# SwiGLU activations of an FFN turned in 32x32 blocks by VectorE and placed through DRAM, instead of by TensorE

## The reference, cut to what matters

```python
mix = jnp.concatenate([ret, moba], axis=-1) @ w_out[layer]
x = x + rmsnorm(mix, post_mix_norm[layer])
h = rmsnorm(x, pre_ffn_norm[layer])
f = (jax.nn.silu(h @ w_gate[layer]) * (h @ w_up[layer])) @ w_down[layer]
x = x + rmsnorm(f, post_ffn_norm[layer])
```

## Time and profile before

| | |
|---|---|
| median of 3 runs | 305.52 us (305.44 to 305.65) |
| profiled execution | 305.34 us, of it a span of 303.5 us |
| mean granted TensorE clock | 0.997 |
| TensorE busy | 98% of the span |
| VectorE, ScalarE busy | 61%, 51% |
| DMA | 58.35 MB, mean 192 GB/s |

### The profile page before, as it was taken

How to read it: one execution, slowest core, us unless ns; L and a number is a source line. 1 busy time by engine, 2 the same in 40 slices (tenths; PEclk the granted TensorE clock), 3 DMA queues, 4 the chain that set the end, 5 groups by cost and what they waited for, 6 DMA issues and landing times.

```text
span 303.5 us, 4145 instructions
## 1 busy us (share of the span) xinstructions
PE 296.3 (98%) x1440; PEld 240.2 (79%) x1440; DVE 183.9 (61%) x273; ACT 155.5 (51%) x255; POOL 12.0 (4%) x20
## 2 busy tenths in 40 slices
PE   8999999999999999999999999999999999999992
PEld 3788877787888888887888888888888888888881
DVE  2867466796877879797456464546355464551146
ACT  4989476736482747495253353544352443630331
POOL 0030000000020013200000000000000000000001
PEclk9999999999999999999999999999999999999998
DMA  6999986218627441669846454654746454600003
GB/s 189 404 408 381 409 353 203 74 31 302 199 94 265 122 168 59 219 204 384 304 148 211 159 197 143 209 190 160 253 139 243 155 219 132 212 6 0 0 2 138
DMA packets 17545, 58.35 MB, mean 192 GB/s; under 512 B 2003, under 2 KB 2556, under 8 KB 17532
## 3 DMA queue, kind: packets, MB, share of 16 engines
q1 hardware_dynamic: 17136, 57.06, 53.4%
q0 software_dynamic: 304, 1.06, 1.0%
q10 hardware_dynamic: 92, 0.05, 0.1%
HBM read 57.10 MB, written 1.06 MB: 192 GB/s over the span
## 4 chain that ended last, share of the span: by engine, by line
PE 87%; DVE 7%; DMA 2%; ACT 1%; issue 1%; SPq 0%; DVEq 0%; POOL 0%; ACTq 0%
PE bank L978 26%; PE bank L980 26%; PE bank L979 26%; PE bank L988 3%; DVE w_lo L887 3%; DMA xT<-in_xt 2%; PE bank L1018 1%; PE bank L1022 1%; PE bank L1026 1%; PE bank L1087 1%; PE bank L1132 1%; DVE d_lo L894 1%; PE bank L997 1%; DVE res L969 1%; DVE res L963 1%
## 5 line engine op out<-in xcount | busy, mean ns | idle before, releaser
L978 PE MATMUL bank<-w_hi,a_hi 128*128 128x512 f32 x256 | 101.0, 395 | 0.0
L980 PE MATMUL bank<-w_hi,a_lo 128*128 128x512 f32 x256 | 99.9, 390 | 0.0
L979 PE MATMUL bank<-w_lo,a_hi 128*128 128x512 f32 x256 | 99.6, 389 | 0.0
L978 PEld LDWEIGHTS bank<-w_hi,a_hi 128*128 128x128 f32 x256 | 48.1, 188 | 10.4 <-issue 0.7
L980 PEld LDWEIGHTS bank<-w_hi,a_lo 128*128 128x128 f32 x256 | 48.0, 188 | 10.2
L979 PEld LDWEIGHTS bank<-w_lo,a_hi 128*128 128x128 f32 x256 | 48.1, 188 | 9.8
L887 DVE TENSOR_TENSOR w_lo<-raw,w_hi 128x1024 fp32r<-128x1024 f32 x40 | 48.1, 1245 | 7.9 <-ACT w_hi L610 7.9
L694 DVE TENSOR_TENSOR w_lo<-raw,w_hi 128x1024 fp32r<-128x1024 f32 x32 | 37.9, 1222 | 12.8 <-ACT w_hi L460 12.8
L625 ACT ACTIVATE sil<-bank,rstd 128x256 f32<-128x256 f32 x22 | 10.4, 475 | 62.3 <-PE bank L980 60.1
L610 ACT ACTIVATE w_hi<-raw 128x1024 fp32r<-128x1024 f32 x40 | 40.1, 1052 | 0.0
L902 DVE SCALAR_TENSOR_TENSOR hid<-bank,rstd,sil 128x256 f32<-128x256 f32 x22 | 10.6, 484 | 46.3 <-ACT sil L625 46.3
(11 more groups left out here) (107 smaller groups left out, 260.4 us busy)
## 6 DMA issues: line engine op xcount, KB each, us to landing
raw<-in_w_gu SPq DMA_DIRECT2D x44, 512.0 KB, 4.3
raw<-in_w_dn SPq DMA_DIRECT2D x22, 512.0 KB, 4.2
raw<-in_w_in SPq DMA_DIRECT2D x20, 512.0 KB, 8.2
raw<-in_w_out SPq DMA_DIRECT2D x8, 512.0 KB, 3.8
raw<-in_w_in SPq DMA_DIRECT2D x8, 256.0 KB, 5.7
xs<-in_x SPq DMA_DIRECT2D x2, 512.0 KB, 8.2
bias<-bias_row POOLq DMA_DIRECT2D x1, 1024.0 KB, 10.2
out<-res SPq DMA_DIRECT2D x4, 256.0 KB, 2.1
```

Of the source, the lines that this page charges most:

```text
L978: pe.matmul(acc, hi, wh, start=first, stop=False)
L979: pe.matmul(acc, hi, wl, start=False, stop=False)
L980: return pe.matmul(acc, lo, wh, start=False, stop=last)
```

## The change

The turn of `hid` is taken from TensorE for groups 0 to 9; group 10, the last, still turns on TensorE (`turn_hidden`, `last_h_high`, `last_h_low`).

For the others VectorE follows each `hidden` by a transpose of the 128x256 tile in blocks of 32x32 into `hid_sq`, 128 partitions by 4 column chunks by 2 tiles by 64. When both tiles are there, SP stores `hid_sq` to the DRAM scratch `h_rows` (one transfer of 256 KB, 128 rows of 2 KB), waits for it, and loads it back into `hid_T` with four transfers of 64 KB, each to 32 partitions, in pieces of 512 B (`store_squares`, `load_turned`). Then ScalarE makes `h_hi` and VectorE `h_lo` for both token tiles at once from SBUF, 128x512 (`h_high`, `h_low`), where before each made two of 128x256 from PSUM. `down` of either tile waits for this one `h_lo`. The rows of `w_down` are laid out on the host in the order in which the blocks arrive.

The orders of the engines: on ScalarE and VectorE the high and low part of group g-1 stand in group g behind the three units ahead of silu (`hidden`) of tile 0; in group 1 they stand just ahead of silu and `hidden` of tile 1. On SP the store of group g-2 stands between the loads of `w_gu` for group g and those of `w_dn` for group g-1, the four loads behind the latter. Gate and up alternate between bank01 and bank45, since bank45 is needed for turns only at the end, and gate_up(g) waits for `hidden` of group g-2 where it waited for that of g-1.

```diff
-            def h_hi_part(g, t):
-                act.wait_ge(h_turned[t], g + 1)
+            def h_high(g):
+                act.wait_ge(hT_loaded, 16 * Q * g + 16 * Q)
                 if not (isinstance(g, int) and g == 0):
-                    wait_down(act, g - 1, t)
-                act.activation(h_hi[:, t, :, :], pt(g)[:, t, 0:FG].rearrange("p (b i) -> p b i", i=P),
-                               ACT.Copy).then_inc(hhi_ready[t], 1)
+                    wait_down(act, g - 1, 1)
+                act.activation(h_hi[:, :, :, :].rearrange("p t j (q i) -> p (t j) q i", i=B),
+                               hid_T[:, :, :, :].rearrange("p q n i -> p n q i"), ACT.Copy
+                               ).then_inc(hhi_ready, 1)
...
+            def store_squares(g):
+
+                sp.wait_ge(sq_ready, NT * g + NT)
+                sp.dma_start(h_rows, hid_sq[:, :, :, :].rearrange("p q t c -> p q (t c)")).then_inc(sq_stored, 16)
+
+            def load_turned(g):
+
+                sp.wait_ge(sq_stored, 16 * g + 16)
+                row = NT * DN * B
+                for q in range(Q):
+                    sp.dma_start(hid_T[q * B:(q + 1) * B, :, :, :].rearrange("p q n i -> p q (n i)"),
+                                 bass.AP(h_rows.tensor, q * row, [[Q * row, B], [B * Q * row, Q], [1, row]])
+                                 ).then_inc(hT_loaded, 16)
+
             def group(g, n0):
 
                 for s in range(GU):
                     load(gu_n(g, s), (n0 + s) % RAW, w_gu[GU * g + s])
+                if not (isinstance(g, int) and g == 1):
+                    store_squares(g - 2)
                 for j in range(DN):
                     load(dn_n(g - 1, j), (n0 + GU + j) % RAW, w_dn[DN * (g - 1) + j])
+                if not (isinstance(g, int) and g == 1):
+                    load_turned(g - 2)
...
+                if not last:
+                    dve.wait_ge(hid_ready[t], g + 1)
+                    if not (isinstance(g, int) and g == 0):
+                        dve.wait_ge(sq_stored, 16 * g)
+                    dve.transpose(hid_sq[:, :, t, :], hid[:, t, :].rearrange("p (q c) -> p q c", q=Q)
+                                  ).then_inc(sq_ready, 1)
+
+            def h_low(g):
+                dve.wait_ge(hhi_ready, g + 1)
+                dve.tensor_tensor(h_lo[:, :, :, :].rearrange("p t j (q i) -> p (t j) q i", i=B),
+                                  hid_T[:, :, :, :].rearrange("p q n i -> p n q i"),
+                                  h_hi[:, :, :, :].rearrange("p t j (q i) -> p (t j) q i", i=B).bitcast(F32),
+                                  ALU.subtract).then_inc(hlo_ready, 1)
...
-            def turn_hidden(g, t):
-                pe.wait_ge(hid_ready[t], g + 1)
-                if not (isinstance(g, int) and g == 0):
-                    pe.wait_ge(hlo_ready[t], g)
-                turn(pt(g)[:, t, :], hid[:, t, :], DN, h_turned[t])
+            def turn_hidden(t):
+                pe.wait_ge(hid_ready[t], NF)
+                turn(pt[:, t, :], hid[:, t, :], DN, h_turned[t])
 
             def down(g, t, g0, last=False):
 
-                pe.wait_ge(hlo_ready[t], g + 1)
+                pe.wait_ge(hlo_ready, g + 1 + (t if last else 0))
...
-            def first_hidden(s):
-                if s == 1:
-                    for t in range(NT):
-                        turn_hidden(0, t)
-
-            def group(g, g0):
+            def group(g, g0, last=False):
                 for t in range(NT):
-                    gate_up(g, t, g0, hook=first_hidden if g0 == 1 and t == 1 else None)
+                    gate_up(g, t, g0)
                 down(g - 1, 0, g0 - 1)
-                for t in range(NT):
-                    turn_hidden(g, t)
+                for t in range(NT if last else 0):
+                    turn_hidden(t)
                 down(g - 1, 1, g0 - 1)
```

More of the change, by code:

```diff
@@ L54 @@
 MASKED = 1e30
+B, Q = 32, 4
 REV = 2 * P + S // 2
@@ L164, in hybrid_layer, with pg @@
         ph = bank45
[L166 to L170, removed]
+        def pg(g0):
+            return bank45 if g0 % 2 else bank01
+        pt = bank45
         pf = [bank67, bank23]
@@ L251, in hybrid_layer @@
         h_turned = [sem(f"h_turned{t}") for t in range(NT)]
-        hhi_ready = [sem(f"hhi_ready{t}") for t in range(NT)]
-        hlo_ready = [sem(f"hlo_ready{t}") for t in range(NT)]
+        sq_ready = sem("sq_ready")
+        sq_stored = sem("sq_stored")
+        hT_loaded = sem("hT_loaded")
+        hhi_ready = sem("hhi_ready")
+        hlo_ready = sem("hlo_ready")
         dn_done = sem("dn_done")
@@ L619, in hi_dn, with silu @@
                                ).then_inc(hi_ready, 1)
-            def silu(g, t):
+            def silu(g, t, g0):
                 wait_gate_up(act, g, t)
@@ L662, in _ @@
             wait_factor(act, X1_, 0)
-            silu(0, 0)
+            silu(0, 0, 0)
             x1_squares(1)
             wait_factor(act, X1_, 1)
-            silu(0, 1)
+            silu(0, 1, 0)
             for j in range(DN):
@@ L673, in _ @@
             group(NF - 1, NF - 1, more=False)
-            h_hi_part(NF - 1, 1)
+            for t in range(NT):
+                last_h_high(t)
             for t in range(NT):
@@ L895, in lo_dn, with hidden, last_h_low @@
                                   ALU.subtract).then_inc(lo_ready, 1)
-            def hidden(g, t):
+            def hidden(g, t, g0, last=False):
                 dve.wait_ge(sil_ready[t], g + 1)
                 if not (isinstance(g, int) and g == 0):
-                    dve.wait_ge(h_turned[t], g)
-                dve.scalar_tensor_tensor(out=hid[:, t, :], in0=pg(g)[:, t, FG:2 * FG],
+                    dve.wait_ge(sq_ready, NT * g - NT + t + 1)
+                dve.scalar_tensor_tensor(out=hid[:, t, :], in0=pg(g0)[:, t, FG:2 * FG],
                                          scalar=rstd[:, X1_, t:t + 1], in1=sil[:, t, :],
                                          op0=ALU.mult, op1=ALU.mult).then_inc(hid_ready[t], 1)
[L906 to L909, removed]
+                if not last:
[10 more added lines that the diff above has]
+                                  ALU.subtract).then_inc(hlo_ready, 1)
+            def last_h_low(t):
+                dve.wait_ge(hhi_ready, NF + t)
+                dve.tensor_tensor(h_lo[:, t, :, :], pt[:, t, 0:FG].rearrange("p (b i) -> p b i", i=P),
+                                  h_hi[:, t, :, :].bitcast(F32), ALU.subtract).then_inc(hlo_ready, 1)
             def group(g, g0, more=True):
-                if g0 > 1:
-                    h_lo_part(g - 1, 1)
                 ahead = 1 if g0 == 1 else GU - 1
@@ L917, in group @@
                         lo_gu(g + 1, s, g0 + 1)
-                hidden(g, 0)
-                if g0 == 1:
-                    for t in range(NT):
-                        h_lo_part(0, t)
+                if g0 > 1:
+                    h_low(g - 1)
+                hidden(g, 0, g0, last=not more)
                 if more:
@@ L924, in group @@
                         lo_gu(g + 1, s, g0 + 1)
-                hidden(g, 1)
+                if g0 == 1:
+                    h_low(0)
+                hidden(g, 1, g0, last=not more)
                 for j in range(DN):
                     lo_dn(g, j, g0)
-                h_lo_part(g, 0)
             residual(0)
@@ L942, in _ @@
                                   ).then_inc(x1_ready[1], 1)
-            hidden(0, 0)
+            hidden(0, 0, 0)
             factor(X1_, 1, 12)
-            hidden(0, 1)
+            hidden(0, 1, 0)
             for j in range(DN):
@@ L952, in _ @@
             group(NF - 1, NF - 1, more=False)
-            h_lo_part(NF - 1, 1)
+            for t in range(NT):
+                last_h_low(t)
             dve.wait_ge(gf_loaded, 16)
@@ L1258, in _ @@
                 group(g + 1, 3)
-            group(NF - 1, NF - 1)
+            group(NF - 1, NF - 1, last=True)
             down(NF - 1, 0, NF - 1, last=True)
@@ L1303, in _laid_out @@
     up = a("w_up")[0].reshape(GU, KPU, P, NF, FG)
+    w_down = a("w_down")[0]
+    in_squares = w_down[:FG * (NF - 1)].reshape(NF - 1, Q, DN, B, D).transpose(0, 2, 1, 3, 4)
     return {
```

35 lines of the change are left out of this document (21 added, 14 removed).

## The result

| | before | after |
|---|---|---|
| median of the runs | 305.48 us (305.11 to 305.65, 4 runs) | 307.88 us (307.56 to 308.11, 4 runs) |
| ratio | | 1.0081 (95% interval 1.0069 to 1.0093) |
| profiled execution | 305.34 us, span 303.5 | 307.75 us, span 305.8 |
| mean granted clock | 0.997 | 0.985 |

The changed kernel is 0.8% slower. It lies inside the forecast's range (303.4 to 308.6), and on the side to which 0.48 of the chance was given, but the forecast itself was 305.3, no change. It is the rival of the clock that came true, with a longer stall than I reckoned.

What follows compares the result with a forecast made beforehand. TensorE, busy 98% of the span, was taken to bound the kernel through its number of instructions. From 305.34 us, 4.8 less for turns and 4.6 more for group 0's stall gave 305.1, forecast as a 305.3 us median, range 303.4 to 308.6.

Steps and rivals of the forecast that it cites:

- the rival of the clock: Group 0's stall: the clock halves while TensorE waits, losing 1.9 us; 307.2 us (306.6 to 309); chance 0.32.
- What the turns cost: TensorE, ten groups: removing turns saves 0.44 us in each of nine and 0.86 in group 1, together 4.8 us.
- The work off TensorE: VectorE and ScalarE: 20 transposes of 0.45 us mostly fit idle stretches; high and low parts take 0.60 and 0.69 us.
- The wait in the loop: Groups 2 to 9: h through DRAM is ready at 162.3, needed at 167.8, 5.5 us to spare.
- The wait at group 0: Before down(0): h's loads queue behind the second down load, so TensorE stands still 4.6 us (ends 2.9 and 6.4).
- The sum: Whole kernel: 305.34 - 4.8 + 4.6 = 305.1 us, forecast as 305.3 because the median is 0.2 above the profiled run.
- the stall with the clock kept: Group 0: stall near 4.6 us without a clock fall; chance 0.40 (0.12 faster, 0.26 same, 0.02 slower).
- The second rival: Group 0: h's loads served beside the weight loads, stall near 2.9 us, 303.6 us; stall under 4.0, clock kept: 0.14.

Runs made afterwards that it cites:

- the kernel whose stall is some 2.2 us: Change as made, with group 0's loads of h ahead of the down weights and its h_lo behind one low part, not three: 303.16 us, ratio 0.9931.
- the last run on ScalarE's queue: Change as made, with group 0's h loaded from ScalarE's queue and SP issuing nothing behind the down loads until h is there: 307.42 us, ratio 1.0071.

## Why the prediction was wrong

**What the turns cost**: right. 0.44 us per group were read; the loop's groups take 16.39 us on average where they took 16.87, 0.48 less. At group 1 0.86 were read; with group 0's turns on TensorE and no fall of the clock, its two downs take 5.47 us instead of 6.36, 0.89 less. The doubled turns give the same price. The forecast summed 4.8 us; by the account it is 3.8 + 0.4 + 0.9 = 5.1.

**The work off TensorE**: right. The transpose takes 0.446 us (0.45 taken), h_hi 0.63 (0.60), h_lo 0.69 (0.69); the first transposes fit where they were said to.

**The wait in the loop**: right. No down but the first waits. The low part of h is ready 3.5 to 6.4 us ahead of its down, where 5.5 were forecast.

**The wait at group 0**: the mechanism right in each link, the term too small. Store landed after 2.0 us (2.1), loads of h issued at 132.0 to 133.4 (131.9 to 133.0). Then two terms fell short: the second down load landed after 5.0 us, not 4.4, and h 1.3 us behind it, not 0.9. I took the 4.4 from another place; the load's own row said 4.7, and in the three traces of experiments in which no load of group 0's h stands behind it (group 0's turns on TensorE, the same with gf late, turns done twice) it takes 4.9, 5.1 and 5.2. So the 5.0 needs no cause in the change. For h I took 256 KB at 305 GB/s; its pieces passed at some 170 GB/s (nine tenths of 256 KB in 1.4 us). The stall was 5.5 us instead of 4.6, inside its stated ends of 2.9 and 6.4.

**The clock**: here the forecast failed. The sum has the stall's 4.6 us and puts the clock's loss at nothing. I had put the stall with the clock kept at 0.40 and the fallen clock at 0.32, because the one row at the end of the program shows the clock 4.1 us after the last matmul still granted. I read this as a threshold just under the stall. It is none: the clock fell 2.5 us after the last matmul's start in the profile after (133.61 to 136.1), 2.4 in the run with h ahead, and in three of ten executions of the kernel whose stall is some 2.2 us; in the last run on ScalarE's queue it fell only after 5.6. The mean clocks of all four runs after (0.985 to 0.990) show the fall each time. Its price was sized right (1.9 forecast, 1.77 here, 1.65 and about 2 in the runs that part it).

The section of the Trainium skill's page "TensorE: Matmul & The Clock Gate" that I had named with that rival held: TensorE waited for a DMA within a stream of matmuls, and the granted clock went from 1.00 to 0.50. The trace's end was the weaker witness.

**The sum** then came to +2.4 where -0.2 was forecast: the stall 0.9 more, the clock 1.8, the start 0.2, the turns -0.3. The second rival, loads that overtake, did not come true: the packets of h began only when most of those of the down loads had started. Two of the four loads landed 0.4 and 0.1 us ahead of the second down load, but the last one, on which the stall hangs, 1.3 us behind it, and a second queue was worse. What decides about this change is one place of eleven; with that place left as it was, the change is worth 4.8 us.

## What to carry to other kernels

When a step that every iteration makes is moved to a longer path, price the first iteration by itself: the cover there (5.1 us) had little to do with the loop's (15.2 us), and keeping the old path for that one iteration turned a loss of 0.8% into a gain of 1.6%. Count a TensorE wait with the clock's loss on top, unless other matmuls fill it: here, by the mean clocks, it fell in every execution of the kernels with a stall of 3.8 us or more in the trace and nothing to fill it, and in three of ten at some 2.2 us. When a stall is shortened, look at what stands ahead of the waiting instruction in each queue on the way: here it was the DMA queue, then VectorE's order.

## What the hardware showed that I had not expected

- The clock's fall comes at very different distances from the last matmul. From its start: 2.5 us in the profile after, 2.4 with h ahead, 3.9 with one load instead of four, 4.3 and 5.6 in the two runs on ScalarE's queue; 3.6 us at the end of the program after (299.73 to 303.35), 4.0 at the end of the kernel before, 5.4 at the end of the run with 22 matmuls without use. One distance read from a trace is no threshold. After, it stayed low for 6.8 us, of them 3.6 with TensorE running; in the run with an earlier low part for 3.4 us.
- Four loads of 64 KB took 2.0 us each from SP's queue with nothing ahead, 3.9 to 4.5 behind two loads of down weights, 4.4 to 5.1 from ScalarE's queue beside those two alone, and 4.3 to 9.9 there with gf and gate and up loads issued among and behind them.
- The landing of a 512 KB load in a full queue was 5.0 us in one profiled execution and 6.2 in another with the same order of transfers. The change as made scatters by 0.6 us in four executions, the same with 22 matmuls by 2.8 in seven, and with one load by 4.2 in seven, where the kernel before scatters by 0.8 or less in any batch. Only one execution of each was traced, so the scatter isn't explained; of the slowest one (310.4 us, with one load), 2.2 us lie in the program's start.
